# Decay scans behind the sixth tile's eviction, two rotations in banks of their own, two groups of value transposes a step sooner

## The reference, cut to what matters

```
def _mixer(h, l, P, past_k, past_v, s_gla0, s_ret0):
    z = h @ P['w_in'][l]                                  # 3344 columns: 27 tiles
    a_lr, gq, gk, gv, gr, dq, dk, dv, rq, rk, rv, rg = jnp.split(z, offs, axis=-1)
    log_a = jax.nn.log_sigmoid((a_lr @ P['w_gla_a2'][l] + P['b_gla_a'][l])) / GLA_TAU
    o_a, s_gla = _gla_chunked(q_a, k_a, v_a, log_a, s_gla0)       # needs cumsum of log_a
    o_d = _diff_attention(q_d, k_all, v_all, pos, jnp.arange(past_len + t), lam)
    q_r = _rotary(rq, pos)
    k_r = _rotary(rk, pos) * DK_R ** -0.5
    o_r, s_ret = _retention_chunked(q_r, k_r, v_r, s_ret0)
    out = jnp.concatenate([o_a, o_d, o_r], axis=-1) @ P['w_out'][l]
    return out, k_rows, v_rows, s_gla, s_ret
```

## Time and profile before

| | |
|---|---|
| median of 3 runs | 1423.31 us (1422.4 to 1423.97) |
| the profiled execution's own time | 1423.22 us |
| its span | 1421.4 us, mean granted TensorE clock 0.989 |
| PE matmul busy | 1370.1 us, 96% of the span, 9649 instructions |
| DVE, ACT, POOL busy | 57%, 44%, 9% |
| the chain that ended last | PE 86%, DVE 5%, DMA 3%, ACT 2% |

### The profile page before, as it was taken

The page is one execution under the profiler, slowest core; times in us unless marked ns, Lnnn a source line. Parts: engine busy times, 40 slices in busy tenths (PEclk is TensorE's granted clock), DMA queues, the critical chain, the costliest instruction groups (busy, mean ns, idle before and its releaser), DMA issues.

```text
span 1421.4 us, 24734 instructions
## 1 busy us (share of the span) xinstructions
PE 1370.1 (96%) x9649; PEld 1332.1 (94%) x9649; DVE 811.5 (57%) x1224; ACT 625.3 (44%) x987; POOL 129.7 (9%) x129
## 2 busy tenths in 40 slices
PE   6999999979999999999999999998899999999998
PEld 6999999968899999999999999998778999999998
DVE  4655544677655675554466555346865467655442
ACT  4444434543354554443454444345334455444333
POOL 2000000351000200000020000013400002000000
PEclk9999999999999999999999999999999999999999
DMA  5755555533233355545545554554223344555552
GB/s 150 204 163 163 159 160 152 144 83 90 78 112 98 92 159 150 151 143 148 156 118 149 148 148 141 153 168 104 75 77 90 100 119 117 150 148 148 142 147 74
DMA packets 351770, 187.34 MB, mean 132 GB/s; under 512 B 6316, under 2 KB 348600, under 8 KB 351704
## 3 DMA queue, kind: packets, MB, share of 16 engines
q1 hardware_dynamic: 348368, 177.49, 44.3%
q0 software_dynamic: 2496, 7.93, 1.6%
q10 hardware_dynamic: 840, 0.99, 0.3%
HBM read 182.07 MB, written 4.33 MB: 131 GB/s over the span
## 4 chain that ended last, share of the span: by engine, by line
PE 86%; DVE 5%; DMA 3%; ACT 2%; issue 1%; DVEq 1%; POOL 1%; ACTq 0%; SPq 0%; POOLq 0%
PE ps L613 26%; PE ps L615 25%; PE ps L614 25%; DVE scores L1415 1%; DVE w_l L492 1%; PE ps L676 1%; PE ps L898 1%; DMA raw<-in_w_in_dram 1%; PE ps L908 1%; DMA raw<-in_ffn_w_up_dram 1%; PE ps L669 1%; PE ps L919 1%; PE ps L801 1%; PE ps L872 1%; DMA raw<-in_w_out_dram 0%
## 5 line engine op out<-in xcount | busy, mean ns | idle before, releaser
L613 PE MATMUL ps<-xn_l,w_h 128*128 128x320 f32 x1840 | 582.3, 316 | 1.9 <-DVE xn_l L1253 1.5
L615 PE MATMUL ps<-xn_h,w_h 128*128 128x320 f32 x1840 | 571.1, 310 | 0.0
L614 PE MATMUL ps<-xn_h,w_l 128*128 128x320 f32 x1840 | 571.0, 310 | 0.0
L492 DVE TENSOR_TENSOR w_l<-raw,w_h 128x1024 fp32r<-128x1024 f32 (+1 forms) x340 | 410.8, 1210 | 181.7 <-ACT w_h L483 181.6
L483 ACT ACTIVATE w_h<-raw 128x1024 fp32r<-128x1024 f32 (+1 forms) x342 | 353.2, 1035 | 270.4 <-DMA raw<-in_ffn_w_down_dram 129.1
L613 PEld LDWEIGHTS ps<-xn_l,w_h 128*128 128x128 f32 x1840 | 347.5, 189 | 11.1 <-issue 4.1
L614 PEld LDWEIGHTS ps<-xn_h,w_l 128*128 128x128 f32 x1840 | 347.6, 189 | 0.8 <-issue 0.2
L615 PEld LDWEIGHTS ps<-xn_h,w_h 128*128 128x128 f32 x1840 | 347.4, 189 | 0.0
L613 PE MATMUL ps<-hid_l,w_h 128*128 128x320 f32 x704 | 217.9, 310 | 0.0
L614 PE MATMUL ps<-hid_h,w_l 128*128 128x320 f32 x704 | 217.9, 309 | 0.0
L615 PE MATMUL ps<-hid_h,w_h 128*128 128x320 f32 x704 | 217.8, 309 | 0.0
(11 more groups left out here) (226 smaller groups left out, 1192.2 us busy)
## 6 DMA issues: line engine op xcount, KB each, us to landing
raw<-in_ffn_w_up_dram SPq DMA_DIRECT2D x176, 512.0 KB, 3.8
raw<-in_ffn_w_down_dram SPq DMA_DIRECT2D x64, 448.0 KB, 3.8
raw<-in_w_in_dram SPq DMA_DIRECT2D x54, 512.0 KB, 3.8
raw<-in_ffn_w_down_dram SPq DMA_DIRECT2D x32, 512.0 KB, 4.0
raw<-in_w_out_dram SPq DMA_DIRECT2D x16, 512.0 KB, 4.0
const<-in_tables_dram POOLq DMA_DIRECT2D x8, 272.0 KB, 4.4
x_in<-in_x_prompt_dram SPq DMA_DIRECT2D x1, 1024.0 KB, 3.9
scores<-in_cache_diff_k_dram POOLq DMA_DIRECT2D x2, 512.0 KB, 5.3
```

The lines of the kernel that those rows point to most:

```text
L492: dve.tensor_tensor(w_l[s][:, 0:cols], raw[s][:, 0:cols], w_h[s][:, 0:cols], ALU.subtract).then_inc(w_lo, 1)
L613: pe.matmul(out, w_h[s][:, w], xl, start=first, stop=False)
L614: pe.matmul(out, w_l[s][:, w], xh, start=False, stop=False)
L615: return pe.matmul(out, w_h[s][:, w], xh, start=False, stop=last)
```

## The change

Four edits, the same in both layers. (1) `decay` is a step of its own behind tile 5 (the sixth); `minus` stays behind tile 4. (2) `rot0` and `rot1` leave bank 3 and its order; they use banks 6 and 7, wait for `abs` and `minus` (readers of bank 7), and `level0` waits for `rot1` on DVE where it waited for `minus`. (3) `tok4` moves from the middle of tile 16 to stand right behind `tok0` in the middle of tile 15. (4) `tok5` moves from the middle of tile 20 to ahead of it. No computation is added or removed.

```diff
-    tile_steps(4) + [("logit",)] + tile_steps(5) + tile_steps(6) + [("past", 0), ("past", 1), ("tok", 8), ("rot", 0), ("weight", 0)]
+    tile_steps(4) + [("logit",)] + tile_steps(5) + [("decay",)] + tile_steps(6) + [("past", 0), ("past", 1), ("tok", 8), ("rot", 0), ("weight", 0)]
...
-    + [("att_s", 0)] + P8[15][:1] + [("tok", 0)] + P8[15][1:]
-    + [("att_s", 1), ("att_a", 0), ("ret_s", 1)] + P8[16][:1] + [("tok", 4)] + P8[16][1:]
+    + [("att_s", 0)] + P8[15][:1] + [("tok", 0), ("tok", 4)] + P8[15][1:]
+    + [("att_s", 1), ("att_a", 0), ("ret_s", 1)] + P8[16]
...
-    + [("att_t", 3), ("att_s", 5), ("att_a", 4)] + P8[20][:1] + [("tok", 5), ("att_o", 3)] + P8[20][1:]
+    + [("att_t", 3), ("att_s", 5), ("att_a", 4), ("tok", 5)] + P8[20][:1] + [("att_o", 3)] + P8[20][1:]
...
-            dve += ["minus", "decay"]
+            dve.append("minus")
+        elif kind == "decay":
+            dve.append("decay")
             pool += ["dist0", "dist1"]
...
-SHARED = [(kind, "" if not arg else arg[0]) for kind, *arg in SCHEDULE if kind in READER]
+SHARED = [(kind, "" if not arg else arg[0]) for kind, *arg in SCHEDULE if kind in READER and (kind, *arg) not in (("rot", 0), ("rot", 1))]
+ROT_BANK = (6, 7, 3, 3)
...
                     else:
                         after(pe, l, "act", "kct1")
-                        after(pe, l, "dve", "minus")
+                        after(pe, l, "dve", "rot1")
...
                 elif kind == "rot":
                     pe.wait_ge(evac, l * GROUPS + G_MIX + RQ + n + 2)
-                    shared_free(l, kind, n)
-                    mark("pe", pe.matmul(bank3[:, 0:T], C("rot"), z[:, RQ + n, :], start=True, stop=True), f"rot{n}")
+                    if n >= 2:
+                        shared_free(l, kind, n)
+                    else:
+                        after(pe, l, "act", "abs")
+                        after(pe, l, "dve", "minus")
+                    mark("pe", pe.matmul(ps[:, ROT_BANK[n], 0:T], C("rot"), z[:, RQ + n, :], start=True, stop=True), f"rot{n}")
...
                          "minus")
+                elif kind == "decay":
                     dve.drain()
                     after(dve, l, "act", "softplus")
```

More of the change, by code:

```diff
@@ L558, in _ @@
                     n = arg[0] if arg else None
-                    if kind == "logit":
+                    if kind == "decay":
                         dist(l, 0)
@@ L1470, in mixer_step @@
                     dve.drain()
-                    dve.tensor_tensor(t, bank3[:, 0:T], C("sin"), ALU.mult)
+                    dve.tensor_tensor(t, ps[:, ROT_BANK[n], 0:T], C("sin"), ALU.mult)
                     dve.tensor_tensor(zt, zt, C("cos"), ALU.mult)
```

## The result

The changed kernel took 1407.68 us (median of 4 runs, 1407.29 to 1408.09), the kernel before 1423.32 (4 runs on the same chip): a ratio of 0.99, interval 0.9883 to 0.9916. It is faster, by more than the range of the prediction allowed: 15.6 us where 9.9 were forecast, 1407.7 where the range began at 1410.5. The profiled execution of the changed kernel took 1408.09 us.

A forecast was written before the change was run, and what follows sets the result against it. PE, busy 96%, was taken to bound the kernel, so only its idle waits could be won back. Gains of 3.3 + 0.6 us (layer 0) and 5.4 + 0.6 (layer 1), 9.9 together, took 1423.22 to 1413.3; range 1410.5 to 1417.3.

The forecast's parts named there:

- The decay scans (edit 1): Scans moved behind tile 5: not delayed, with 1.4 us to spare, and PE no longer waits before `kct1`.
- `level0` at 6.8, `level1` at 9.9: Start of both mixers, us behind the decay scan; gain at `level1` 4.7 in layer 0, 5.5 in layer 1.
- the sum: Whole kernel: 3.3 + 0.6 us in layer 0 and 5.4 + 0.6 in layer 1, together 9.9 us faster.
- So I take 17.4 for both: `level1` to `level5`: 17.4 us in both layers, as `rot2` falls into POOL's `qk4`; before, 15.98 and 17.27.
- Edit 3, 0.6 per layer: Tiles 15 and 16: 1.82 us wait and 0.52 of transposes go, 1.2 wait before `tok4` comes; 0.6 gained.
- Edit 4, nothing: Tile 20: the 0.78 us wait before `att_o3` stays, as ACT's order is unchanged; gain 0, bound 0.78 per layer.
- the 12.7 that was the end of the range: Largest gain in the range: 4.6 + 6.8 + 1.2 = 12.6, with rounding 12.7 us, giving 1410.5.
- (b): `level1` to `level5`: no collision, both layers take 15.98 us; 12.7 us gained, 1410.5; chance 0.13.
- (a): Levels: the wait before `level1` stays or POOL and DVE collide once more per layer; 5.7 to 6.9 gained; chance 0.19.
- (c): Mixer start: ACT's `hi` of tile 11 waits for a late transfer, holding `tok9` 4 us; 1421 to 1423; chance 0.03.
- (d): Slower: `level0` waits for a `rot1` not advanced, 0.6 us later per layer, plus `tok4`'s wait; 1426.8; chance 0.02.

## Why the prediction was wrong

**The decay scans (edit 1)** were not delayed, and the wait before `kct1` vanished, as forecast. The edit without the second gains nothing that can be measured, which the prediction did not ask: the queue for bank 3 took over (3.20 us).

**`level0` at 6.8, `level1` at 9.9.** Measured 6.81 and 6.82, 9.64 and 9.65. The course up to `rot1` held, its long last operation (1.41) with it, and the order of the collision behind it too: `dist2`, then DVE's `lo` of tile 11, then `qk1`. But `qk1` ended 9.49 behind the scan and not 9.76 (299.7 - 289.94), and `level1` came without a wait: 0.25 sooner per layer.

**Two steps of the sum failed**: the 17.4 us from `level1` to `level5`, and the clock outside the mixers' starts, which the sum put at nothing without a reason. The first alone would have left the result in the range: 1423.2 less the 12.1 of the two mixers is 1411.1. What carried it out is the second, 3.0 us of the pair.

**The first step that failed: "So I take 17.4 for both".** From `level1` to `level5` it took 16.50 and 16.49 us, 0.9 less, in both layers and in every later run of this start (16.46 to 16.51). The forecast put the third rotation at the very start of `qk4`, at 307 with `qk4` from 306.9 to 308.5: 17.1 and 17.0 behind the scan, so that an operation of it would be held for nearly the whole product. In the trace `qk4` runs from 304.05 to 305.60, 15.96 to 17.51 behind the scan, and the rotation begins at 304.78, 16.69 behind it. Its operations lost 0.27 to the tail of `qk4` and 0.36 to the distance behind it (0.75 and 0.85 for the 0.48 and 0.49 of an operation alone): 0.6 where I had put 1.4. POOL was 1.0 us ahead of the course that I had given it: 0.3 at `qk1`, 0.4 at `qk2`, 0.8 at `qk3`, 1.0 at `qk4`. Three distances took 0.72 to 0.76 where I had put 0.86 each, 0.4 in all, and most of the rest came at `qk1` and `qk3`, the two products that stood behind a `lo`. So small errors added up over seven operations, while the loss by a collision turns on 0.3 us. That DVE's work sets this distance, collisions included, holds in the main: taking 1.4 us of it out shortened it by 1.00 and 1.28. With the 0.25 of `level1`, `level5` came 26.14 behind the scan for 27.3: 2.3 us over the two layers.

**Edit 3, 0.6 per layer.** Measured 0.59 and 0.61 (from `level5` to tile 20, 65.10 and 65.14 before, 64.51 and 64.53 after); the wait of 1.2 before `tok4` as forecast. **Edit 4, nothing**: right, the wait of 0.8 is ACT's order, and it vanished when this order was changed.

**The second step that failed, what the sum left out.** 9.9 and 2.3 make 12.2, the 12.1 that the traces show inside the two mixers. The other 3.0 of 15.1 are stretches at half clock at 256, 468 and 952 us that the profiled execution of before had and that of after had not, less one at 415. They come and go in executions of one kernel: in the repeat of the changed kernel they stand at 256, 417, 464, 707 and 949 again, the distance from its `level0` to its `level5` being the same to 0.01, and it took 1413.38 us where the first took 1408.09. On the means the change is worth 1422.1 - 1409.0 = 13.1 us, with an error of 0.7. The 12.1 of the pair and the fall of the clock that the execution of before was spared at the start of layer 0 (0.9) make 13.0 of it. How much is clock can be estimated another way: 16.9 us missed before and 12.4 after, at 0.75 us for each, is 3.4 of the 13.1. What lets the clock fall at 256, 468, 707 or 949 us in one execution and not in another stays open. So the forecast was 3.2 us short on the means and 5.7 on the medians, and 2.5 of the latter is the spread of few runs: the changed kernel's first four lay 1.3 below its mean, those of before 1.2 above. On the means the gain of 13.1 lies within its error of the 12.7 that was the end of the range. A range for medians of four runs should have held 2 to 3 us on each side for this alone.

**The rivals.** (b), no collision, was nearest, and still 2.8 us above the median, 1.5 above the mean; neither of its two distances (15.98) came about. (a), given back at the levels, did not: the wait before `level1` is gone. (c) did not: `tok9` waited 0.90, for the copy of `tok8` as forecast (0.6). (d) did not: `level0`'s new wait on `rot1` is there (1.21), but `level0` stands 3.7 and 4.5 us sooner behind the scan than it did.

## What to carry to other kernels

Two waits in a row on the same engine hide each other: removing one gained 1.2 us, the other 3.4, both together 11.9, by estimate 4 of it through the clock. So a single edit's null result says nothing of the pair. Where two engines hold each other up, the loss turns on a few tenths of a microsecond, and a chain followed is off by more than that after some operations: sum up with the middle of the cases, not with the worst one. Place a copy by the order of the engine that makes it, not of the one that needs it: two copies moved ahead of an exponential that waits for a maximum gained what moving the transposes alone did not.

## What was unexpected of the hardware

The granted clock fell to half in pieces that each cost 1.7 us, at places where nothing in PE's instructions differs between executions: at 256 us in some (PE busy 4.99 of 5.00 us before and clock 0.66; the changed kernel's first execution 1.00), at 707 and 949 in others. They explain most of the spread of 12 us among 79 executions of the kernel before, by the 0.75 us for each microsecond of granted clock that is missing. What decides them is open; splitting the small matmuls doubled the loss behind them in layer 0.

Who waits in a collision of DVE and POOL turns on tenths. In the changed kernel (the two rows below) `dist0` began 0.22 us ahead of DVE's `lo`, took its 0.61, and the `lo` 1.48; in the kernel with the moved zeroing the two began a hundredth apart (291.16 and 291.17), and `dist0` took 1.69, the `lo` its 1.22. (The Trainium skill, "SBUF — State Buffer", "SBUF: two separate sides", has one of the two hold the port for its whole instruction; these rows agree: where the one held ended at 290.74 and at 292.85, waiting for all of the other gives 290.87 and 293.00.)

```profile
289.04 0.61 POOL L523 TENSOR_TENSOR wgt<-decay 128x256 f32<-128x256 f32 x1 [21.04 <-DVE decay L1408]
```

```profile
289.26 1.48 DVE L495 TENSOR_TENSOR w_l<-raw,w_h 128x1024 fp32r<-128x1024 f32 x1
```
